# Moving a memory branch (norm, keys, values of two layers) to the top of a three-network program

## The chip, the cores and the metric

The kernel runs on one core of one Trainium2 chip. The metric is device microseconds of one execution; the time before is the median of three. A core has TensorE (matrix products into PSUM, in fp32 or fp32r here), VectorE (DVE), ScalarE (ACT), GpSimd (POOL, which here only starts transfers) and SyncE (SP, which only starts weight transfers). The engines run their own instruction lists in order and meet only at semaphores.

## What is computed

Three small transformer networks stand one behind the other on x, 256 tokens by 1024 channels. The second one has two layers (a fox layer of forget attention, then a conv layer), and each of them also attends to a memory `mem` that doesn't depend on x:

```python
def second_block(x, mem, norm_mix, norm_mem, ...):
    h = x
    for i in range(DEPTH):                      # 2
        u = rms_norm_2(h, norm_mix[i])
        m = rms_norm_2(mem, norm_mem[i])
        mk, mv = jnp.split(m @ w_mem_kv[i], 2, axis=-1)     # 1024 x 512
        ...                                     # fox (i = 0) or conv (i = 1) mix of u, and mq
        mem_out = memory_attention(mq, mk, mv, g_mq[i], g_mk[i])
        h = h + jnp.concatenate([mix, mem_out], axis=-1) @ w_out
        ...
```

`rms_norm_2(mem, g)` is mem times one factor for each token times a gain for each channel, so the token factors are the same for both layers. The first network has adaptive norms: its shifts, scales and gates come from `c` through a matrix `ada_w` of 36 groups of 512 columns, four quarters (512 KB each) a group; the first layer's first norm needs groups 0 to 3.

## The kernel before

x lies in SBUF with channels on the partitions, as 8 tiles of 128 by 256 tokens. Every fp32 product is made as three fp32r matmuls (high times high, high times low, low times high). A chunk is 1 MB of weights, 128 by 2048. SP loads chunks into a ring of 4; ScalarE copies one into `whi` (L1619), VectorE subtracts to get `wlo` (L2409), TensorE multiplies with both, 48 matmuls of 256 columns for a chunk. `split_to` runs up to 3 chunks ahead of the one in use.

A norm is a chain over three engines: ScalarE squares x into T (`squares`), TensorE sums over channels with a column of ones as 32 one-column matmuls (`stat`), ScalarE takes the root (`root`), VectorE the reciprocal (`rinv`), TensorE turns it to a row, ScalarE copies it out (`rows_out`), TensorE broadcasts it over the partitions (`bcast`), VectorE scales (`scaled_rows`), ScalarE makes the high halves (`halves`), VectorE the low ones (`lower`). `heat` puts matmuls on a tile `warm` without a use for their result in between: 4 in the statistics, 18 after the broadcast. Ahead of a feed-forward network each engine waits at a fence for the others.

The program is one fixed order for each engine, written out in the classes Pe, Act, Dve, Pool and Sp. `network()` (L431) does `start`, then `need_mod(0, 1)`, which runs adaLN groups 0 to 3: VectorE sums the weighted rows of each quarter as the GpSimd queue's three buffers (`rring`, "raws") bring them (`ada`, L2391), TensorE adds over partitions (`ada_sums`, 4 products of one column, 8 matmuls), VectorE adds the bias. Then come the first network, `final_norm`, `fox`, a feed-forward network, `conv_layer`, `moe`, `moba` and `cross`.

Around the change: in `fox` and `conv_layer` the GpSimd queue waits for the fence (`after`), then loads a table `ex` and `mem` into the working area AF; the engines run a norm of mem, keys (`lin`) and values (`lin_nat`), and the keys' own factors for each head (`pair_stat`, `head_norm`). In fox the statistics of x stand behind these products, without `heat`; in the conv layer the whole norm of x does. Then x's own chunks begin. In `moba` the table `ex` is loaded a third time together with two others.

Of the kernel before, what the change touches and what calls it, by code (L numbers as in the profile page):

```python
# [28 lines left out]
def const_table():  # L29
# [105 lines left out]
LOADS = ("cst", "small", "x", "pos", "ex0", "mem0", "oh", "ex1", "mem1", "ex3", "rot3", "pool3", "mem3")  # L135
# [34 lines left out]
class Net:  # L170


    def __init__(self, nc, ctx, dram, out, count):
# [21 lines left out]
        self.warm = sb("warm", [P, S], F32R)  # L195
# [8 lines left out]
        self.moes = sb("moes", [P, 8, 16])  # L204
# [22 lines left out]
    def lay(self):  # L227
# [3 lines left out]

        af = Arena(self.AF)
        self.h_CU, self.h_GB = af.take(4, S), af.take(4, S)
        self.h_q0, self.h_kv0 = af.take(2, S), af.take(2, S)
        self.h_Cs, self.h_Sn, self.h_ang, self.h_kk = [af.take(S) for _ in range(4)]
        self.h_qn, self.h_qr = af.take(4, S), af.take(2, S)
        self.h_kn, self.h_vn = af.take(4, S), af.take(2, 512)
        self.h_posi = af.take(S)
        ar = Arena(self.AR)
        ar.n = af.n  # L240
        self.hqh, self.hql, self.hkh, self.hkl = ar.take(2, S), ar.take(2, S), ar.take(1, S), ar.take(1, S)
        assert ar.n <= self.AF.shape[1]
# [8 lines left out]
        self.n_pt, self.n_cs, self.n_gT = af.take(512), af.take(2, 16), af.take(S)  # L251

        af = Arena(self.AF)
        self.x_ex = af.take(1536)[0:24, :]
        keep = af.n
        self.x_q = af.take(6, S)
        af.take(512)
        af.n = keep
        self.m_xm = af.take(8, S)
        self.m_mk, self.m_mv = af.take(2, S), af.take(2, 256)  # L260
        after = af.n
# [4 lines left out]
        af.n = after  # L266
# [10 lines left out]
        af.take(1536)  # L277
# [95 lines left out]
class Side:  # L373
# [58 lines left out]
    def network(self):  # L432
        self.start()
        for l in range(2):
            for j in range(2):
                key = ("ff", l, j)
                self.need_mod(l, 7 if j else 1)
                self.norm((key, "n"), self.N.X, ("mod", l, 2 * j))
# [15 lines left out]
        self.finish_all()  # L454

# [9 lines left out]
class Pe(Side):  # L465
# [93 lines left out]
    def heat(self, n):  # L559

        b = self.take(("heat", self.heats))
        self.heats += 1
        w = self.N.warm
        for _ in range(2 * n):
            self.mm(b[:, 0:S], w[:, 0:P], w[:, :], True, True)

    def norm(self, key, X, which, n=8, T=None):
        T = self.N.T if T is None else T
        self.stat(key, [T[:, k, :] for k in range(n)], heat=2)
        self.rows_of(key, 1)  # L570
        self.bcast(key, self.N.ones[0:1, :])
        self.heat(9)
# [488 lines left out]
    def head_norm(self, key, x, n):  # L1061
        N = self.N
        self.rinv(key, [N.T[:, k, :] for k in range(n)], G=2 * n)
        for k in range(n):
            self.bcast(key, N.x_ex[0:2 * n, k * P:(k + 1) * P], ("bc", k), k == n - 1)
# [11 lines left out]
    def pair_bcast(self, key):  # L1077
        for k in range(2):
            self.bcast(key, self.N.x_ex[0:4, k * P:(k + 1) * P], ("bc", k), k == 1)

    def mem_kv(self, i):
        N = self.N
        self.norm(("mem", i), N.m_xm, ("V", "norm_mem_2", i))
        self.lin(("mem", i, "k"), [(0, "w_mem_kv_2", (i,), 0, 8, (0, 256))], ("mem", i))
        self.lin_nat(("mem", i, "v"), [(0, "w_mem_kv_2", (i,), 0, 8, (256, 256))], ("mem", i))
        self.mark(("mem", i, "in"))
        self.wait_ge("ld_ex0" if i == 0 else "ld_ex1", 16)
        self.head_norm(("mk", i), N.m_mk, 2)

    def mem_heads(self, i, mq, mqkey):  # L1090
        N = self.N

        def ready(h):
            self.wait_ge("dve", (mqkey, "h", h // 2))
            self.wait_ge("dve", (("mk", i), "h", h // 2))
        return Heads(("mem", i), MEM, at=12, q=lambda h: [mq[rows(h), h // 2, :]], k=lambda h: [N.m_mk[rows(h), h // 2, :]],
                     v=lambda h, kb: N.m_mv[:, kb, h * 64:h * 64 + 64], ready=ready,
                     vready=lambda h: self.wait_ge("act", ("mem", i, "v", 1)))
# [2555 lines left out]
```

## Time and profile before

| | us |
|---|---|
| median of 3 runs (3596.22 to 3599.97) | 3598.55 |
| the profiled execution | 3605.26 |
| its span, first to last instruction | 3603.4 |
| TensorE busy | 3291.7 (91%) |
| VectorE busy | 2306.6 (64%) |
| ScalarE busy | 1685.5 (47%) |

Times in the rows below are microseconds from the start of the span unless they say ns. In a timeline a row is a start, a duration, an engine, a line of the kernel, an operation, what it writes and reads, and how often; in brackets stands how long the engine had been idle before it and what ended that. A row of a stretch gives its length, the busy us and instructions of PE, PEld, DVE, ACT and POOL, the granted clock, the DMA engines' busy share and GB/s; a row of a queue its packets, MB and share. A busy TensorE counts overlapping matmuls as one stretch. The granted clock is a share of 2.4 GHz: 1.00 or 0.50, in between for a stretch with both.

### The profile page before, as it was taken

What the parts mean: (1) busy time and instruction counts of PE and PEld (TensorE: products, weight loads), DVE (VectorE), ACT (ScalarE), POOL (GpSimd) and SP (SyncE); (2) the same over time, 40 slices, a digit from 0 to 9 for tenths busy, and PEclk for the clock granted to TensorE, in tenths of its full rate; (3) what the DMA queues carried; (4) which work ended last, traced back from release to release, by engine and by line L of the source; (5) the groups of instructions that cost most, each with busy time, mean ns of one, the idle gap of its engine ahead of it and who ended that gap; (6) DMA issues with size and microseconds to landing.
All of it is one profiled execution on the core that took longest, in us unless ns stands there. A gap on an engine that the chain in (4) does not pass through costs nothing. (4 is left out here: it accounts for less than half of the span.)

```text
span 3603.4 us, 49674 instructions
## 1 busy us (share of the span) xinstructions
PE 3291.7 (91%) x21314; PEld 2982.2 (83%) x21314; DVE 2306.6 (64%) x2636; ACT 1685.5 (47%) x1866; POOL 86.9 (2%) x168
## 2 busy tenths in 40 slices
PE   3998999999989989999826899999999999999999
PEld 3998899999879978799815778778778778889899
DVE  4775577675445543444385678778788787654575
ACT  2334333434324344343302567667667666534453
POOL 1010001010000000000000000000000000000000
PEclk9998899999879978899766899999999999998999
DMA  6784378585214632145311589789798898633253
GB/s 225 263 292 154 119 264 291 208 286 189 95 47 164 211 110 97 59 176 182 110 38 37 192 309 358 303 320 343 292 346 321 304 356 308 246 106 106 100 182 117
DMA packets 112604, 741.05 MB, mean 206 GB/s; under 512 B 12588, under 2 KB 12588, under 8 KB 32224
## 3 DMA queue, kind: packets, MB, share of 16 engines
q1 hardware_dynamic: 89424, 651.21, 49.0%
q0 software_dynamic: 22928, 86.27, 7.0%
q8 instruction: 184, 3.01, 0.3%
q14 instruction: 68, 0.56, 0.0%
HBM read 736.38 MB, written 1.05 MB: 205 GB/s over the span
## 5 line engine op out<-in xcount | busy, mean ns | idle before, releaser
L2409 DVE TENSOR_TENSOR wlo<-ring,whi 128x2048 fp32r<-128x2048 f32 x620 | 1419.3, 2291 | 562.6 <-ACT whi L1619 562.2
L1619 ACT ACTIVATE whi<-ring 128x2048 fp32r<-128x2048 f32 x620 | 1184.8, 1913 | 347.0 <-issue 221.7
L473 PE MATMUL ps<-whi,AR 128*128 128x512 f32 x2692 | 873.9, 400 | 0.1
L473 PE MATMUL ps<-hh,whi 128*128 128x256 f32 x2768 | 798.3, 288 | 9.1 <-DVE wlo L2409 6.8
L473 PE MATMUL ps<-hl,whi 128*128 128x256 f32 x2768 | 791.6, 286 | 0.0
L473 PE MATMUL ps<-hh,wlo 128*128 128x256 f32 x2768 | 791.1, 286 | 0.0
L473 PEld LDWEIGHTS ps<-whi,AR 128*128 128x128 f32 x2692 | 506.6, 188 | 118.4 <-issue 1.6
L473 PEld LDWEIGHTS ps<-hh,whi 128*128 128x128 f32 x2768 | 538.5, 195 | 11.5 <-DVE wlo L2409 7.1
L473 PEld LDWEIGHTS ps<-hl,whi 128*128 128x128 f32 x2768 | 538.3, 194 | 0.5
L473 PEld LDWEIGHTS ps<-hh,wlo 128*128 128x128 f32 x2768 | 537.5, 194 | 0.6
L473 PE MATMUL ps<-wlo,AR 128*128 128x512 f32 x1346 | 532.6, 396 | 0.0
L472 PE MATMUL ps<-AR,whi 128*128 128x256 f32 x2112 | 377.6, 280 | 0.0
L472 PEld LDWEIGHTS ps<-AR,whi 128*128 128x128 f32 x2112 | 325.0, 189 | 0.0
L473 PEld LDWEIGHTS ps<-wlo,AR 128*128 128x128 f32 x1346 | 253.7, 188 | 55.7
L472 PE MATMUL ps<-AR,wlo 128*128 128x256 f32 x1056 | 297.3, 282 | 0.0
L472 PEld LDWEIGHTS ps<-AR,wlo 128*128 128x128 f32 x1056 | 198.9, 188 | 0.0
L2391 DVE SCALAR_TENSOR_TENSOR cv<-rring,ca,cv 128x512 f32<-128x512 f32 x238 | 178.8, 751 | 22.8 <-DMA rring<-in_r 7.9
L1607 ACT ACTIVATE AR<-gf 128x512 fp32r<-128x512 f32 x66 | 41.8, 633 | 252.1 <-DVE gf L2382 252.1
L1607 ACT ACTIVATE cv<-ps,att 128x256 f32<-128x256 f32 (+1 forms) x144 | 60.5, 425 | 208.8 <-DVE att L2400 208.8
L473 PE MATMUL ps<-AF 64*128 64x128 f32 (+4 forms) x456 | 138.6, 415 | 3.1 <-DVE AF L2391 1.8
L482 PE MATMUL ps<-cst,cv 128*128 128x128 f32 x228 | 42.9, 306 | 103.3 <-ACT cv L1607 95.4
L1607 ACT ACTIVATE gs<-ps 128x512 f32<-128x512 f32 x55 | 32.8, 597 | 209.0 <-PE ps L473 209.0
(197 smaller groups left out, 3492.4 us busy)
## 6 DMA issues: line engine op xcount, KB each, us to landing
ring<-in_w SPq DMA_DIRECT2D x620, 1024.0 KB, 4.9
rring<-in_r POOLq DMA_DIRECT2D x151, 512.0 KB, 4.9
AF<-in_mem POOLq DMA_DIRECT2D x3, 1024.0 KB, 5.2
X<-in_x POOLq DMA_DIRECT2D x1, 1024.0 KB, 13.5
AF<-in_cst POOLq DMA_DIRECT2D x1, 1024.0 KB, 6.0
y_out<-X SPq DMA_DIRECT2D x1, 1024.0 KB, 3.9
cst<-in_cst POOLq DMA_DIRECT2D x1, 478.0 KB, 7.5
AF<-in_cst POOLq DMA_DIRECT2D x3, 144.0 KB, 3.0
```

What stands on the lines that cost most here:

```text
L472: return self.e.matmul(out, l, r, start=start, stop=stop, skip_group_check=True)
L473: return self.e.matmul(out, l, r, start=start, stop=stop)
L482: return self.e.transpose(out, in_, self.N.ident[0:n, 0:n])
L1607: self.e.activation(out, in_, f, **kw).then_inc(*self.up(*keys))
L1619: self.e.activation(N.whi[:, c % HB, :], N.ring[:, c % RING, :], ACT.Copy).then_inc(N.sem["hi"], 1)
L2391: self.e.scalar_tensor_tensor(out=out, in0=a, scalar=s, in1=b, op0=op0, op1=op1).then_inc(*self.up(*keys))
L2409: self.e.tensor_tensor(N.wlo[:, c % HB, :], N.ring[:, c % RING, :], N.whi[:, c % HB, :].bitcast(F32), ALU.subtract).then_inc(N.sem["lo"], 1)
```

## The change

The memory branch of both layers leaves `fox` and `conv_layer` and stands in a new `memory()` at the top, between `start` and the first layer. It takes adaLN groups 0 to 3 in, in an order of its own, and the token factors of the first layer's norm, whose scaling (`scale`) stays where the norm was. mem is squared and its factors made once. Keys and values of both layers stay in the last 2048 columns of AF until they are used. GpSimd loads mem ahead of the first raws and x behind them, SP waits for mem ahead of the first chunk. The table `ex` becomes a part of the constants that always stay (2 heads' pairs are enough), `warm` shrinks to 128 columns and is read twice, and some tiles move or share a place. The core of the diff:

```diff
+LOADS = ("cst", "small", "x", "mem", "pos", "oh", "rot3", "pool3", "mem3")
-        self.warm = sb("warm", [P, S], F32R)
+        self.warm = sb("warm", [P, P], F32R)
-        self.moes = sb("moes", [P, 8, 16])
+        self.moes = self.att[:, :, :, :].rearrange("p a b c -> p (a b c)")[:, 0:128].rearrange("p (a b) -> p a b", a=8)
     def network(self):
         self.start()
+        self.memory()
...
-                self.norm((key, "n"), self.N.X, ("mod", l, 2 * j))
+                (self.scale if (key, "n") == FIRST else self.norm)((key, "n"), self.N.X, ("mod", l, 2 * j))
# TensorE
-            self.mm(b[:, 0:S], w[:, 0:P], w[:, :], True, True)
+            self.mm(b[:, 0:S], w[:, :], w[:, :].unsqueeze(1).to_broadcast([P, 2, P]), True, True)
+    def factors(self, key, tiles, heat=2):
+        self.stat(key, tiles, heat=heat)
+        self.rows_of(key, 1)
+        self.bcast(key, self.N.ones[0:1, :])
+    def memory(self):
+        N = self.N
+        self.base, self.span = 0, 8
+        for g in range(4):
+            self.ada(g, 0)
+            self.ada(g, 1)
+        self.adan = 4
+        self.factors("mem", [N.s_tm[:, k, :] for k in range(8)], 0)
+        self.ada_sums(0)
+        for i in range(2):
+            self.lin(("mem", i, "k"), [(0, "w_mem_kv_2", (i,), 0, 8, (0, 256))], ("mem", i), hh=N.s_mh, hl=N.s_ml)
+            self.lin_nat(("mem", i, "v"), [(0, "w_mem_kv_2", (i,), 0, 8, (256, 256))], ("mem", i), hh=N.s_mh, hl=N.s_ml)
+            self.mark(("mem", i, "in"))
+            self.ada_sums(1 + i)
+            self.pair_stat(f"mk{i}")
+            self.pair_rows(f"mk{i}")
+            self.pair_bcast(f"mk{i}")
+        self.factors(FIRST, [N.T[:, k, :] for k in range(8)])
+        self.ada_sums(3)
+        self.base, self.span = 4, 4
     def fox(self):
...
-        self.norm(("mem", 0), N.m_xm, ("V", "norm_mem_2", 0))
-        self.lin(("mem", 0, "k"), [(0, "w_mem_kv_2", (0,), 0, 8, (0, 256))], ("mem", 0))
-        self.lin_nat(("mem", 0, "v"), [(0, "w_mem_kv_2", (0,), 0, 8, (256, 256))], ("mem", 0))
-        self.mark(("mem", 0, "in"))
-        self.wait_ge("ld_ex0", 16)
-        self.pair_stat("mk0")
-        self.stat("fox", [N.T[:, k, :] for k in range(8)])
-        self.pair_rows("mk0")
-        self.rows_of("fox", 1)
-        self.bcast("fox", N.ones[0:1, :])
-        self.pair_bcast("mk0")
+        self.norm("fox", N.X, ("V", "norm_mix_2", 0))
     def conv_layer(self):
-        self.mem_kv(1)
         self.norm("cv", N.X, ("V", "norm_mix_2", 1))
# ScalarE
+    def memory(self):
+        N = self.N
+        self.adan = 4
+        self.squares("mem", N.s_xm, 8, lambda k: self.wait_ge("ld_mem", 16), N.s_tm)
+        self.root("mem", 1024)
+        self.rows_out("mem")
+
+        def keys(i):
+            self.copy_out(("mem", i, "k"), N.m_mk[i])
+            self.pair_squares(f"mk{i}", N.m_mk[i], "act", ("mem", i, "k"))
+            self.copy_nat(("mem", i, "v"), lambda tb: N.m_mv[i][:, tb, :])
+
+        self.halves(("mem", 0), N.s_tm, N.s_mh, 8)
+        self.split_to(1)
+        keys(0)
+        self.wait_ge("mm", ("mem", 0, "in"))
+        self.halves(("mem", 1), N.s_tm, N.s_mh, 8)
+        self.split_to(3)
+        self.root("mk0", 64, 4)
+        self.rows_out("mk0", 4)
+        keys(1)
+        self.squares(FIRST, N.X, 8, lambda k: self.wait_ge("ld_x", 16), N.T)
+        self.root("mk1", 64, 4)
+        self.rows_out("mk1", 4)
+        self.rinv(FIRST, 8 * P)
+        self.chunks += 4
# VectorE
     def start(self):
-        self.wait_ge("ld_x", 16)
+    def memory(self):
+        N = self.N
+        self.adan = 4
+
+        def scaled(i):
+            self.wait_ge("mm", ("mem", "bc"))
...
+        self.ada(0, 0)
+        self.wait_ge("ld_mem", 16)
+        self.rinv("mem")
+        self.ada(0, 1)
+        scaled(0)
+        self.lower(("mem", 0), N.s_tm, N.s_ml, N.s_mh, 8)
+        self.split_to(0)
+        self.ada(1, 0)
+        self.split_to(1)
+        scaled(1)
+        self.ada_sums(0)
+        self.ada(1, 1)
+        self.wait_ge("mm", ("mem", 0, "in"))
+        self.lower(("mem", 1), N.s_tm, N.s_ml, N.s_mh, 8)
+        self.split_to(3)
+        self.ada_sums(1)
+        self.ada(2, 0)
+        self.rinv("mk0", 4)
+        self.ada(2, 1)
+        self.pair("mk0", N.m_mk[0], N.V("g_mk_2", 0))
+        self.ada_sums(2)
+        self.ada(3, 0)
+        self.rinv("mk1", 4)
+        self.ada(3, 1)
+        self.pair("mk1", N.m_mk[1], N.V("g_mk_2", 1))
+        self.rinv(FIRST)
+        self.wait_ge("ld_x", 16)
+        self.ada_sums(3)
+        self.chunks += 4
# VectorE, hybrid
+        self.wait_ge("act", ("hy", "cos"))
         self.lower("hykvn", N.T[:, 1:2, :], N.hkl, N.hkh, 1)
# GpSimd
+        self.load("mem", N.s_xm, N.dram["mem2"])
+        self.raw_to(RAW)
         self.load("x", N.X[:, :, :], N.dram["x"])
-        self.raw_to(RAW)
     def fox(self):
         self.after()
-        self.table("ex0", N.x_ex, N.cat["ex"][0], 1536, 24)
-        self.load("mem0", N.m_xm, N.dram["mem2"])
     def conv_layer(self):
-        self.after()
-        self.table("ex1", N.x_ex, N.cat["ex"][0], 1536, 24)
-        self.load("mem1", N.m_xm, N.dram["mem2"])
+        self.fence()
     def moba(self):
-        self.table("ex3", N.x_ex, N.cat["ex"][0], 1536, 24)
# SP
+        self.wait_ge("ld_mem", 16)
```

## Rows read from the trace of the kernel before

**Rows 1.** The page's busy tenths of TensorE in 40 slices of 90 us.
```profile
PE   3998999999989989999826899999999999999999
```

**Rows 2.** Timeline of the start, all engines.
```profile
16.02 2.19 ACT L1607 ACTIVATE T<-X 128x512 f32<-128x512 f32 x4 [4.82 <-DMA X<-in_x]
...
19.21 0.49 DVE L2386 TENSOR_SCALAR cv<-rring,ca 128x512 f32<-128x512 f32 x1 [18.20 <-DMA rring<-in_r]
...
28.57 4.03 DVE L2391 SCALAR_TENSOR_TENSOR cv<-rring,ca,cv 128x512 f32<-128x512 f32 x5
...
53.35 1.87 PE L473 MATMUL ps<-ones,cv 128*128 128x1 f32 x8 [7.79 <-DVE cv L2391]
...
62.94 0.26 ACT L1607 ACTIVATE st<-ps,cst 128x2 f32<-128x2 f32 x1 [43.44 <-PE ps L472]
...
65.84 3.22 DVE L2391 SCALAR_TENSOR_TENSOR T<-X,gain,ps 128x256 f32<-128x256 f32 x8 [2.44 <-PE ps L473]
...
74.32 8.89 DVE L2409 TENSOR_TENSOR wlo<-ring,whi 128x2048 fp32r<-128x2048 f32 x4 [2.09 <-ACT whi L1619]
...
76.67 0.58 PE L473 MATMUL ps<-hh,whi 128*128 128x256 f32 x1 [6.81 <-DVE wlo L2409]
```

**Rows 3.** DMA queues in 5.5-6, 10-12, 18-20; landing of mem's loads.
```profile
q0 software_dynamic: 16, 0.12, 57.8%
...
q1 hardware_dynamic: 53, 0.43, 52.0%
q0 software_dynamic: 63, 0.39, 46.4%
...
q0 software_dynamic: 233, 0.82, 102.9%
...
DMA to landing us min/median/max: 5.1/5.2/6.9
```

**Rows 4.** Timelines of VectorE, ScalarE and TensorE in the fox layer.
```profile
1286.45 3.22 DVE L2391 SCALAR_TENSOR_TENSOR X<-X,sm,ps 128x256 f32<-128x256 f32 x8 [2.36 <-PE ps L473]
...
1312.46 2.77 DVE L2382 TENSOR_TENSOR hl<-T,hh 128x256 fp32r<-128x256 f32 x8
...
1297.76 2.19 ACT L1607 ACTIVATE T<-AF 128x512 f32<-128x512 f32 x4 [12.61 <-DMA AF<-in_mem]
...
1313.22 0.33 PE L473 MATMUL ps<-hh,whi 128*128 128x256 f32 x1
...
1338.01 0.37 PE L473 MATMUL ps<-hh,whi 128*12 128x256 f32 x1 [2.03 <-DVE hl L2382]
```

**Rows 5.** The same three timelines in the conv layer.
```profile
1718.65 2.73 DVE L2382 TENSOR_TENSOR X<-X,ps 128x256 f32<-128x256 f32 x8
...
1727.85 2.19 ACT L1607 ACTIVATE T<-AF 128x512 f32<-128x512 f32 x4 [11.44 <-DMA AF<-in_mem]
...
1743.29 0.34 PE L473 MATMUL ps<-hh,whi 128*128 128x256 f32 x1
...
1775.45 0.41 PE L473 MATMUL ps<-hh,whi 128*128 128x256 f32 x1
```

**Rows 6.** Timelines of ScalarE and TensorE at the third network's first norm.
```profile
3109.25 2.19 ACT L1607 ACTIVATE T<-X 128x512 f32<-128x512 f32 x4 [5.96 <-DVE X L2382]
...
3122.59 0.33 PE L473 MATMUL ps<-hh,whi 128*128 128x256 f32 x1
```

**Rows 7.** Four stretches: busy time of each engine, granted clock, transfers.
```profile
120.00:140.00 20.00, 20.00 (x169) 19.92 (x169) 15.54 (x18) 7.83 (x6) 2.11 (x4) 1.00 0.81 283
...
76.00:81.00 5.00, 4.33 (x20) 4.34 (x21) 5.00 (x4) 4.90 (x4) 0.00 (x0) 1.00 0.64 236
...
1330.00:1340.00 10.00, 7.22 (x27) 4.51 (x27) 5.85 (x17) 5.97 (x12) 0.00 (x0) 0.50 0.00 0
...
1760.00:1768.00 8.00, 8.00 (x36) 7.35 (x36) 0.96 (x2) 0.79 (x2) 0.00 (x0) 0.50 0.00 0
```

More of the change, by code:

```diff
@@ L264, in lay @@
         self.x_oh = af.take(1536)[0:12, :]
-        af.n = after
+        assert af.n <= free
+        af = Arena(self.AF)
         self.c_U, self.c_acc, self.c_mq = af.take(6, S), af.take(6, S), af.take(2, S)
@@ L564, in heat, with scale @@
         for _ in range(2 * n):
-            self.mm(b[:, 0:S], w[:, 0:P], w[:, :], True, True)
+            self.mm(b[:, 0:S], w[:, :], w[:, :].unsqueeze(1).to_broadcast([P, 2, P]), True, True)
     def norm(self, key, X, which, n=8, T=None):
         T = self.N.T if T is None else T
-        self.stat(key, [T[:, k, :] for k in range(n)], heat=2)
+        self.factors(key, [T[:, k, :] for k in range(n)])
+        self.heat(9)
+    def factors(self, key, tiles, heat=2):
+        self.stat(key, tiles, heat=heat)
         self.rows_of(key, 1)
         self.bcast(key, self.N.ones[0:1, :])
-        self.heat(9)
+    def scale(self, key, X, which):
+        pass
     def final_norm(self):
@@ L1685, in norm, with scale @@
         if which is not None:
-            if which[0] == "mod":
-                self.wait_ge("dve", ("part", which[1], 3 * which[2]))
-            self.halves(key, T, N.hh, n, gain_of(N, which)[1])
+            self.scale(key, X, which, n, T)
+    def scale(self, key, X, which, n=8, T=None):
+        N = self.N
+        if which[0] == "mod":
+            self.wait_ge("dve", ("part", which[1], 3 * which[2]))
+        self.halves(key, N.T if T is None else T, N.hh, n, gain_of(N, which)[1])
     def final_norm(self):
@@ L1996, in fox @@
         self.wait_ge("act", f)
-        self.norm(("mem", 0), N.m_xm, ("V", "norm_mem_2", 0), ready=lambda k: self.wait_ge("ld_mem0", 16))
-        self.wait_ge("dve", (("mem", 0), "h", 7))
-        self.squares("fox", N.X, 8, self.ready_x, N.T)
-        self.chunk()
-        self.copy_out(("mem", 0, "k"), N.m_mk)
-        self.pair_squares("mk0", N.m_mk, "act", ("mem", 0, "k"))
-        self.chunk()
-        self.copy_nat(("mem", 0, "v"), lambda tb: N.m_mv[:, tb, :])
-        self.root("mk0", 64, 4)
-        self.root("fox", 1024)
-        self.rows_out("mk0", 4)
-        self.rows_out("fox")
-        self.wait_ge("mm", ("mem", 0, "in"))
-        self.halves("fox", N.T, N.hh, 8)
+        self.norm("fox", N.X, ("V", "norm_mix_2", 0))
         self.chunk()
@@ L2446, in norm, with scale @@
     def norm(self, key, X, which, n=8):
+        self.rinv(key)
+        self.scale(key, X, which, n)
+    def scale(self, key, X, which, n=8):
         N = self.N
-        self.rinv(key)
         gain, shift = gain_of(N, which)
@@ L2989, in fox @@
         self.wait_ge("dve", f)
-        self.wait_ge("ld_mem0", 16)
-        self.norm(("mem", 0), N.m_xm, ("V", "norm_mem_2", 0))
-        self.chunk()
-        self.chunk()
+        self.norm("fox", N.X, ("V", "norm_mix_2", 0))
         gq = self.scaled(N.V("fox_g_q_2", 0), 20, 0.125)
@@ L2997, in fox @@
         self.wait_ge("dve", self.here())
-        self.rinv("mk0", 4)
-        self.rinv("fox")
-        self.scaled_rows("fox", N.T, N.X, N.V("norm_mix_2", 0), 8, lambda k: ("fox", "n", k))
-        self.wait_ge("mm", ("mem", 0, "in"))
-        self.lower("fox", N.T, N.hl, N.hh, 8)
-        self.pair("mk0", N.m_mk, N.V("g_mk_2", 0))
         self.chunk()
@@ L3450, in ada, with memory @@
         self.use_raws(2)
+    def memory(self):
+        for g in range(4):
+            self.ada(g, 0)
+            self.ada(g, 1)
+        self.adan = 4
     def use_raws(self, n):
@@ L3460, in norm @@
         pass
+    scale = norm
     def final_norm(self):
```

94 lines of the change are left out of this document (35 added, 59 removed).

## The prediction

> **What bounds the kernel now.** I read the busy slices of the page first: TensorE is busy nearly throughout, except in the first slice, 3 tenths of 90 us [rows 1]. So work that leaves TensorE's path later on is a gain, and what matters is whether the start can take it up. The start is read in order of time [rows 2]: x is squared at 16.02, the first adaLN quarter is summed by VectorE at 19.21, four groups of quarters follow, the last 8 small matmuls of a group run at 53.35, and only then does TensorE take the token statistics of the first layer, so that their square root comes at 62.94, the scaling at 65.84 and the first matmul of the network at 76.67. The two later places: the second network's first layer (fox) [rows 4] and its conv layer [rows 5]; in each, a norm of mem, loaded just then, stands ahead of the norm of x. What ends last in both is one serial chain: load, squares (ScalarE), 32 one-column matmuls, root, turn, broadcast, scale, lower halves, first matmul.
>
> **Two prices used throughout.** A 256-column matmul takes 0.118 us at the full rate (169 in 20.00 us) and 0.217 at the low one (20 in 4.33 us) [rows 7]. At 76 to 81 us the granted clock is written as 1.00, yet the spacing is that of 1.2 GHz; where the record says 0.50, in 1760 to 1768, 36 small ones fill 8.00 us [rows 7]. A chunk's 48 matmuls thus take 5.7 us warm; started cold, with 20 at the low rate, 4.3 + 28 x 0.118 = 7.7 us.
>
> **Fox.** Before: x is final at 1286.45 + 3.22 = 1289.7; squares of mem start at 1297.76; its first matmul is at 1313.22; the first matmul on x at 1338.01 [rows 4]. After: squares of x can start at 1289.9 and the same chain follows. From squares to first matmul it takes 15.5 us here (1297.76 to 1313.22), and 13.3 in the third network's first stage, where no transfer is waited for (3109.25 to 3122.59) [rows 6]. TensorE is now idle for less long ahead of it, so I take 14.5: 1304.4, which is 33.6 earlier (bounds 32.6 and 34.8). The 18 warming matmuls, which the old path left out ahead of x, now precede it; the 24 matmuls of the first chunk, begun at 1338 with 0.50 granted [rows 7], run at the full rate: 24 x 0.1 = 2.4, taken (bounds 0 and 2.6). Together 36.0. Next late is nothing new: the four chunks in hand are those for x, split ahead by both engines.
>
> **Conv.** x is final at 1718.65 + 2.73 = 1721.4; mem's squares at 1727.85, its first matmul 1743.29, x's first at 1775.45 [rows 5]. After: squares at 1721.6, plus 13.3 to 15.4, take 14.4: 1736.0, 39.4 earlier; a warmer first chunk adds 0 to 1.1, take 0.5. Together 39.9 (bounds 38.4 and 41.6). The depthwise convolution behind it hangs on these chunks and moves with them.
>
> **The third network** loses one of three table loads, but its first matmul (3122.59) follows the scaling and not a load [rows 6]: nothing. Also nothing: the new addresses; the extra VectorE wait for the cosine in the hybrid layer (ScalarE makes it ahead of the copies that the same step waits for anyway); the gate and router tiles laid on others, with no wait added. The warming matmuls now read 128 columns twice; the same 256 columns pass, taken as equal (see the rivals).
>
> **The start, walked engine by engine.** All this is new and in order on each engine; VectorE: quarters 0-1, 2-3, scale mem, lower, split 0, quarters, split 1, scale mem again, quarters, (mem 0 through TensorE), lower, splits 2-3, quarters, reciprocal of key 0, and so on.
> 1. Loads. The GpSimd queue's first bytes flow at about 5.5 us (0.12 MB by 6) and alone it carries 0.82 MB in 2 us [rows 3]. Constants (now 606 KB), small table and mem are 2.06 MB: 5.0 us, with landing 11.3. The SP queue now waits for this. Sharing gives each queue about half, 0.39 and 0.43 MB in 2 us [rows 3]; so raws 0 to 2 land at 12.5, 13.8, 16.3, x at 21, raw 3, queued behind it, at 23.8; weight chunk 0 near 18.
> 2. Statistics of mem: squares at 11.3; at the low rate 32 of the 36 matmuls that fill 8.00 us [rows 7] take about 7.2, from 11.6 on, so root at 18.8, reciprocal 19.2. VectorE, with quarters 0-1 done by 15.7 (4 steps a pair; 5 steps take 4.03 us [rows 2], so 3.2 a pair), takes quarter 2 to 20.8 and waits for raw 3: 25.4.
> 3. Scale 3.2 [rows 2], lower 2.8 [rows 4], first split 2.2 (four take 8.89 [rows 2]): 33.7. TensorE's keys of layer 0 start at 33.8, cold, 7.7: 41.5; values 5.7: 47.3.
> 4. VectorE meanwhile: pair 36.9, split 39.2, scale 42.4, pair 45.8; it then waits for 47.3. ScalarE's halves and two splits end at 54.0, VectorE's lower at 51.0 and its two splits at 56.6, pair 60.0, reciprocal 60.2.
> 5. TensorE stands from 49 until that reciprocal: its program turns and broadcasts key 0's factors ahead of layer 1. This takes about 3.1 (one factor, root to scale, 62.94 to 65.84 [rows 2], with a second broadcast). Layer 1 starts at 63.3, cold: 7.7 + 5.7 + the group's sums 1.0 (half of the 1.87 at 53.35, as warm) = 77.7.
> 6. VectorE has the sums of group 2 in its order ahead of group 3, and group 2's matmuls stand behind layer 1 on TensorE: it is held from 65 to 77.9. Then a pair 81.1, reciprocal of key 1, turn, broadcast 84.4.
> 7. TensorE now takes x's statistics, cold, 7.8: 92.2; root to broadcast 2.9 [rows 2]: 95.1; the sums of group 3 take 1.9 (53.35), VectorE adds: 97.5. Before, scaling at 65.84 led to the first matmul at 76.67, 10.8 later [rows 2]: the same steps give 108.3.
> So the first layer starts 31.6 later. Bounds: with no wait at all VectorE's own work (16 quarters 24.3, two scalings 6.4, two lowers 5.5, four splits 8.9, small ones 2.5) from 12.5 ends at 60.1, and with step 7's tail without the statistics (some 16) the first matmul would come at 76: a price of 0. At the other end, later raws (3), no warm matmul (4 in the two layers), and slower handovers (2): 41.
>
> **Two pages weighed.** The rows show a 1 MB load landing 5.1 us or more after its issue, and both queues sharing [rows 3]. The Trainium skill (DMA: Bandwidth & Descriptors, the anatomy of one SWDGE transfer) fits a transfer as 2.0 us plus its bytes over 436 GB/s, and says that engines alternate between queues by packet; the second agrees with the rows. By the first, mem would land near 9.2 and the start would cost some 2 us less; the rows decide.
> The rows have TensorE at the low rate when it resumes after standing (0.217 us a matmul from 76 on, 0.50 granted up to 1340 and from 1760 on [rows 7]). The Trainium skill (TensorE: Matmul & The Clock Gate, HAM oscillation) says the same of kernels whose work comes in islands, and advises keeping it together; it speaks against this start, in which layer 0, layer 1 and x's statistics are three islands. Were all three warm, the start would cost about 7 us less.
>
> **Sum.** Removed 36.0 + 39.9 = 75.9; added 31.6; net 44.3 off the profiled 3605.26 (span 3603.4). That execution is 6.7 above the median 3598.55; the difference belongs to stages, so it is taken off the median: 3554.
>
> **Rivals.** (A) Forecast, 3542 to 3568, 0.64. (B) The start is cheaper, about 15: the waits of steps 5 and 6 are shorter, because TensorE or the loads come earlier than I walked. For: VectorE's own work could end at 60. Against: the order of both programs makes these waits. 3598.6 - 75.9 + 15 = 3538; 0.12. (C) The start costs about 50, since the raws and the weights delay each other all through, not only raw 3: 3573; 0.14. (D) The two removed passes hid something, such as weight loads or splits, so that about 50 of the 75.9 come: 3580; it includes the case that the change does not do what it says in one of the layers. Against: the queue is idle there, and both splits run ahead. 0.06. (E) Slower: the warming matmuls, fed now by a repeated 128-column block, take longer. Thirteen blocks of 18 remain right ahead of the first matmul of their stages, in the chain. At 0.217 each, doubled, they cost 3.9 us a block, 51 in all, against 44 gained: slower than before from about 1.9 times their present length, 3605 at double. Against: the same columns pass, and no row shows a pattern slowing a matmul. 0.04.
>
> **Numbers.** About 0.2%, 7 us, is what a measurement can tell. A and B lie below it, C and D nearly all: faster 0.93, same 0.03 (tails of C to E), slower 0.04. The range takes the bounds of A, half of B and most of C's near side: 3540 to 3572.
>
> **What would show it.** In the changed profile: the first matmul on mem near 34, a stand of TensorE of about 11 us before 63 that ends with a reciprocal, VectorE held until about 78, the network's first matmul near 108; fox's first matmul on x 14 to 15 us after the squares, near 1336; conv's near 1732; warming matmuls of the same length. A first network matmul before 95 or after 120 proves the walk wrong, a gap between squares and first matmul over 16 in fox or conv proves the removal wrong.

## The result and the profile after

| | before | changed |
|---|---|---|
| median, us | 3597.39 (3594.31 to 3599.97, 4 runs) | 3547.41 (3538.64 to 3555.22, 4 runs) |
| the profiled execution | 3605.26 | 3542.27 |
| its span | 3603.4 | 3540.4 |
| first matmul of the first network | 76.67 | 105.54 |

The ratio of changed to before is 0.9861, with a 95% interval of 0.9832 to 0.9889: the change saves 50 us by the medians and 63 between the two profiled executions. The forecast was 3554, within 3540 to 3572.

The page of the changed kernel, busy tenths of TensorE in 40 slices of 89 us, to be held against [rows 1]: the first slice has risen from 3 to 6, since keys and values of both layers run there, and the second has fallen from 9 to 8, since the first network starts inside it.
```profile
PE   6899999999999999999808999999999999999999
```

The timeline of the changed kernel's start, which answers to [rows 2] (start, duration, engine, line, operation, count; in brackets the idle time before and its end). L481, L482, L491, L2402, L2411, L2417, L2429 and L1620 are L472, L473, L482, L2382, L2391, L2397, L2409 and L1607 of before.
```profile
9.49 2.19 ACT L1620 ACTIVATE AF<-AF 128x512 f32<-128x512 f32 x4 [1.23 <-DMA AF<-in_mem]
10.27 6.96 PE L481 MATMUL ps<-ones,AF 128*128 128x1 f32 x32 [10.27 <-ACT AF L1620]
...
17.63 0.17 DVE L2417 RECIPROCAL st<-st 128x2 f32<-128x2 f32 x1 [3.90 <-ACT st L1620]
...
22.00 1.54 DVE L2411 SCALAR_TENSOR_TENSOR cv<-rring,ca,cv 128x512 f32<-128x512 f32 x2 [2.57 <-DMA rring<-in_r]
...
31.61 0.80 PE L482 MATMUL ps<-AR,whi 128*128 128x256 f32 x2 [6.15 <-DVE wlo L2429]
...
57.40 0.59 PE L491 MATMUL ps<-cst,st 128*4 128x128 f32 x2 [10.70 <-DVE st L2417]
...
60.45 0.80 PE L482 MATMUL ps<-AR,whi 128*128 128x256 f32 x2
...
75.55 0.16 DVE L2402 TENSOR_TENSOR mod<-ps,sm 128x4 f32<-128x4 f32 x1 [11.40 <-PE ps L482]
...
81.75 3.57 PE L481 MATMUL ps<-ones,T 128*128 128x1 f32 x16
...
94.71 3.22 DVE L2411 SCALAR_TENSOR_TENSOR T<-X,gain,ps 128x256 f32<-128x256 f32 x8
...
105.54 0.58 PE L482 MATMUL ps<-hh,whi 128*128 128x256 f32 x1 [11.34 <-DVE wlo L2429]
```
What is to be seen: the chain has two long stands of one engine, TensorE's 10.70 ahead of 57.40 and VectorE's 11.40 ahead of 75.55. How much of each is due to the order alone is what the experiments below find out.

The fox layer of the changed kernel, which answers to [rows 4]: final scaling of the first network, squares of x, scaling, first matmul on x.
```profile
1312.55 3.23 DVE L2411 SCALAR_TENSOR_TENSOR X<-X,sm,ps 128x256 f32<-128x256 f32 x8 [2.36 <-PE ps L482]
...
1315.86 2.19 ACT L1620 ACTIVATE T<-X 128x512 f32<-128x512 f32 x4 [4.62 <-DVE X L2411]
...
1329.04 0.41 PE L482 MATMUL ps<-hh,whi 128*12 128x256 f32 x1
```
The same of the conv layer, for [rows 5].
```profile
1700.55 2.73 DVE L2402 TENSOR_TENSOR X<-X,ps 128x256 f32<-128x256 f32 x8
...
1703.36 2.19 ACT L1620 ACTIVATE T<-X 128x512 f32<-128x512 f32 x4 [5.05 <-DVE X L2402]
...
1718.12 0.41 PE L482 MATMUL ps<-hh,whi 128*128 128x256 f32 x1
```
From the final scaling's start to the first matmul on x, fox takes 1329.04 - 1312.55 = 16.5 us, against 1338.01 - 1286.45 = 51.6 before: 35.1 less. From x's last addition to the first matmul on x, conv takes 1718.12 - 1700.55 = 17.6, against 56.8: 39.2 less.

### The profile page after: what moved, and what is told of

Read it like the earlier page. It is cut to its first block, busy times and chain, and to the rows that moved or that the text cites. A ratio compares the mean times of both kernels' runs of the same rounds, so it can differ in the third digit from the quotient of the medians.

```text
span 3540.4 us, 49498 instructions
## 1 busy us (share of the span) xinstructions
PE 3262.7 (92%) x21238; PEld 2953.9 (83%) x21238; DVE 2306.3 (65%) x2635; ACT 1682.4 (48%) x1860; POOL 84.8 (2%) x164
## 4 chain that ended last, share of the span: by engine, by line
PE 78%; DVE 6%; ACT 2%; issue 1%; DMA 0%; DVEq 0%; ACTq 0%; POOLq 0%
PE ps L482 62%; PE ps L481 13%; DVE AF L2411 3%; PE ps L491 2%; DVE wlo L2429 1%; ACT whi L1632 1%; DVE X L2402 0%; DVE hl L2402 0%; DVE AR L3300 0%; DVE T L2402 0%; ACT hh L1620 0%; DVE X L2411 0%; ACT rT L1620 0%; DVE cv L2411 0%; DVE AR L2408 0%
## 5 line engine op out<-in xcount | busy, mean ns | idle before, releaser
L2429 DVE TENSOR_TENSOR wlo<-ring,whi 128x2048 fp32r<-128x2048 f32 x620 | 1419.3, 2291 | 552.2 <-ACT whi L1632 551.9
L482 PE MATMUL ps<-whi,AR 128*128 128x512 f32 (+1 forms) x2756 | 885.5, 397 | 0.0
L482 PE MATMUL ps<-hh,whi 128*128 128x256 f32 (+1 forms) x2736 | 785.6, 287 | 11.5 <-DVE wlo L2429 11.3
L482 PE MATMUL ps<-hl,whi 128*128 128x256 f32 (+1 forms) x2736 | 778.9, 285 | 0.0
L482 PE MATMUL ps<-hh,wlo 128*128 128x256 f32 (+1 forms) x2736 | 778.2, 284 | 0.0
L482 PEld LDWEIGHTS ps<-whi,AR 128*128 128x128 f32 x2756 | 516.3, 188 | 118.3 <-issue 1.6
L482 PE MATMUL ps<-wlo,AR 128*128 128x512 f32 (+1 forms) x1378 | 541.4, 393 | 0.0
L482 PEld LDWEIGHTS ps<-hh,whi 128*128 128x128 f32 (+1 forms) x2736 | 529.2, 193 | 12.6 <-DVE wlo L2429 11.4
L482 PEld LDWEIGHTS ps<-hl,whi 128*128 128x128 f32 (+1 forms) x2736 | 529.3, 193 | 0.3
L482 PEld LDWEIGHTS ps<-hh,wlo 128*128 128x128 f32 (+1 forms) x2736 | 528.5, 193 | 0.3
L481 PE MATMUL ps<-AR,whi 128*128 128x256 f32 x2112 | 378.3, 280 | 0.0
L481 PEld LDWEIGHTS ps<-AR,whi 128*128 128x128 f32 x2112 | 325.5, 189 | 0.0
L482 PEld LDWEIGHTS ps<-wlo,AR 128*128 128x128 f32 x1378 | 259.6, 188 | 55.8
L481 PE MATMUL ps<-AR,wlo 128*128 128x256 f32 x1056 | 297.5, 282 | 0.0
L481 PEld LDWEIGHTS ps<-AR,wlo 128*128 128x128 f32 x1056 | 199.2, 189 | 0.0
L2411 DVE SCALAR_TENSOR_TENSOR cv<-rring,ca,cv 128x512 f32<-128x512 f32 x238 | 178.8, 751 | 25.5 <-DMA rring<-in_r 9.4
L1620 ACT ACTIVATE AR<-gf 128x512 fp32r<-128x512 f32 x66 | 41.8, 633 | 252.3 <-DVE gf L2402 252.3
L1620 ACT ACTIVATE cv<-ps,att 128x256 f32<-128x256 f32 (+1 forms) x144 | 60.6, 426 | 208.4 <-DVE att L2420 208.4
L482 PE MATMUL ps<-AF 64*128 64x128 f32 (+4 forms) x456 | 141.6, 424 | 3.1 <-DVE AF L2411 2.4
L491 PE MATMUL ps<-cst,cv 128*128 128x128 f32 x228 | 42.6, 304 | 101.9 <-ACT cv L1620 93.9
L1620 ACT ACTIVATE gs<-ps 128x512 f32<-128x512 f32 x55 | 32.9, 597 | 209.9 <-PE ps L482 209.9
```

The costliest lines, as they stand in the source:

```text
L481: return self.e.matmul(out, l, r, start=start, stop=stop, skip_group_check=True)
L482: return self.e.matmul(out, l, r, start=start, stop=stop)
L491: return self.e.transpose(out, in_, self.N.ident[0:n, 0:n])
L1620: self.e.activation(out, in_, f, **kw).then_inc(*self.up(*keys))
L2411: self.e.scalar_tensor_tensor(out=out, in0=a, scalar=s, in1=b, op0=op0, op1=op1).then_inc(*self.up(*keys))
L2429: self.e.tensor_tensor(N.wlo[:, c % HB, :], N.ring[:, c % RING, :], N.whi[:, c % HB, :].bitcast(F32), ALU.subtract).then_inc(N.sem["lo"], 1)
```

## Where the time went, by stage

The boundaries are the first network's first matmul, fox's first matmul on x, and the start of one weight split of VectorE near the end of the conv layer, the same one in all kernels; each row is one profiled execution, in us. The last nine, of eight kernels, have the change in fox and conv; they differ from each other by design at the start alone, except the one without warming.

| kernel | to the first matmul | to fox's matmul on x | to the end of conv | to the end |
|---|---|---|---|---|
| before | 76.7 | 1261.3 | 685.4 | 1580.0 |
| before, again | 75.7 | 1254.8 | 684.3 | 1576.9 |
| changed | 105.5 | 1223.5 | 633.1 | 1578.2 |
| changed, again | 104.4 | 1222.1 | 633.3 | 1571.5 |
| sums of group 2 later | 102.9 | 1226.7 | 633.9 | 1575.6 |
| no wait for mem on SP | 110.0 | 1225.7 | 632.6 | 1569.1 |
| key factors behind layer 1 | 96.9 | 1225.2 | 637.0 | 1578.4 |
| x's factors in place | 105.4 | 1219.0 | 639.7 | 1576.3 |
| start reordered | 82.4 | 1220.0 | 640.0 | 1577.7 |
| without mem's work | 68.7 | 1220.9 | 635.8 | 1572.7 |
| without warming in fox | 105.7 | 1222.6 | 641.2 | 1572.5 |

So the start costs 28.9 and the two layers give it back and more; behind the conv layer nothing stands clearly out of the scatter (1569 to 1578, 1575 on average, against 1577 and 1580).

## The experiments

**The theory** is the sum of the prediction: a chain removed in fox and in conv, a chain added at the start whose length is the order of the programs. **The rivals** are that the work at the start costs that much in any order, that the removed passes gave something back (D), that the warming matmuls changed (E), that the place of x's token factors matters, and chance for whatever exceeds the sum.

### The changed kernel and the kernel before, once more

No edit: the changed kernel is timed five times more, and the kernel before as if it were a new one.

> The changed kernel once more, with five rounds, since its four runs lay 17 us apart (3538.6 to 3555.2) where those of before lay 6 apart. Theory S (structure): start 28.9 later, fox 35.0 and 2.6 earlier, conv 40 earlier, 49 in all, so 3548 in the median, and the spread comes from the granted clock in stretches in which TensorE is busy in pieces, such as fox's attention. Then the first matmul of the network stands again at 105.5 and fox and conv give the same lengths to 1 us, while the attention stages differ from the first profile by some us. Theory F (fixed): the 63 us between the first two profiles are all from the change, and the new profile shows the 6.6 us gained inside fox's attention again, and the median goes to 3540.

Measured: 3538.17 (3533.24 to 3539.45, 5 runs) against 3592.5 (3589.63 to 3595.92, 9 runs), ratio 0.985 [0.9837, 0.9864]; span 3531.3. The signs that came are those of theory F, not of S: the median is 3538, and fox's attention, from the first matmul on x, takes 121.6 as in the first profile (121.8). The first matmul of the first network is at 104.42, 1.1 earlier than expected.

> The kernel before, profiled a second time. Its first profile took 130.9 us from fox's first matmul on x to the end of its attention, the changed kernel's two profiles 121.8 and 121.6; 2.6 of the 9.1 are the first chunk at the full clock. Theory S: the other 6.5 are stretches at a low granted clock that come and go, so this profile differs from the first by some us there, without an edit. Theory F: the change removed them by something, then this profile takes 130.9 again to 1 us.

Measured: 3591.51 (8 runs) against 3595.14 (9 runs), ratio 0.9993 [0.9981, 1.0005]; span 3591.8, 11.6 less than that of the first profiled execution, with the same program. The attention of fox is one place where it comes from: 127.2 in place of 130.9, so theory F fails here. Four stretches of it, the first two of before, the other two of before again, which has come to the same place of the program 7.5 us earlier (length, busy us and instructions of PE, PEld, DVE, ACT, POOL, granted clock, DMA share, GB/s):
```profile
1360.00:1380.00 20.00, 20.00 (x161) 18.85 (x159) 9.18 (x10) 9.33 (x14) 0.00 (x0) 1.00 0.40 142
...
1400.00:1420.00 20.00, 20.00 (x126) 17.89 (x124) 7.82 (x12) 9.54 (x19) 0.00 (x0) 0.83 0.18 61
```
```profile
1360.00:1380.00 20.00, 19.54 (x110) 15.63 (x109) 6.73 (x12) 6.78 (x12) 0.00 (x0) 0.81 0.31 106
...
1400.00:1420.00 20.00, 20.00 (x141) 16.86 (x141) 7.63 (x17) 10.09 (x21) 0.00 (x0) 1.00 0.29 106
```
With the same program the granted clock falls below 1.00 in other stretches from execution to execution, though TensorE is busy for 19.5 to 20.0 us of each 20. The changed program does it too: the reordered kernel below, which has the same fox layer, takes 128.2 for this attention. One stretch of it, and the one of the changed kernel at the same distance (60 us) from fox's first matmul on x:
```profile
1362.00:1382.00 20.00, 20.00 (x124) 17.74 (x123) 7.52 (x10) 9.96 (x19) 0.00 (x0) 0.83 0.19 71
```
```profile
1389.00:1409.00 20.00, 20.00 (x142) 16.86 (x141) 8.01 (x12) 9.45 (x20) 0.00 (x0) 1.00 0.29 106
```
So a few us of any difference of two profiles are chance.

### Without mem's work

Keys and values of both layers are constants of 0.5; mem's norm, products and key factors are left out, the rest of the new order stays. TensorE's part of the edit, with its lines on the products joined into one; ScalarE and VectorE lose what belongs to them:
```diff
-        self.factors("mem", [N.s_tm[:, k, :] for k in range(8)], 0)
         self.ada_sums(0)
-        for i in range(2):
-            self.lin(...) ... self.pair_bcast(f"mk{i}")
+        self.ada_sums(1)
+        self.ada_sums(2)
         self.factors(FIRST, [N.T[:, k, :] for k in range(8)])
```


> The memory branch's norm, keys and values are left out altogether (keys and values are set to 0.5, so the attention to memory computes something else); adaLN groups and the first layer's factors stay at the top. It prices the removal apart from the start. Fox and conv should be as in the changed kernel to 1 us. VectorE's quarters run from 10.8 and need some 34 us as before, and root to first matmul follows: first matmul of the network at about 61, 44 earlier than 105.5, so 3503 (3493 to 3513). If the removed passes had hidden something (rival D), or the stages behind take back what they get, it is more than 3515.

Measured: 3510.91 (3499.99 to 3516.1), ratio 0.9779 [0.9764, 0.9794]. Its first network matmul and the wait that I had not counted:
```profile
21.57 1.54 DVE L2381 SCALAR_TENSOR_TENSOR cv<-rring,ca,cv 128x512 f32<-128x512 f32 x2 [6.12 <-DMA rring<-in_r]
```
```profile
68.75 0.58 PE L482 MATMUL ps<-hh,whi 128*128 128x256 f32 x1 [11.33 <-DVE wlo L2399]
```
The start is 7.7 longer than I expected: x, loaded ahead of raw 3, holds VectorE for 6.12, and the next raws for 2.50 and less. The median is 8 above the 3503 expected, within the range given. Two things follow. The stages behind the start take 1220.9 and 635.8, among the values of the kernels with mem's work at the start (1219.0 to 1226.7 and 632.6 to 640.0): nothing of that work is felt later beyond the scatter. And mem's work costs 105.54 - 68.75 = 36.8 in the order that the change has.

### Key factors of layer 0 behind layer 1

TensorE's part; ScalarE's row of layer 0 moves behind the keys of layer 1, and VectorE applies the factors one pair of quarters later.
```diff
+            if i:
+                self.pair_rows("mk0")
+                self.pair_bcast("mk0")
             self.pair_stat(f"mk{i}")
-            self.pair_rows(f"mk{i}")
-            self.pair_bcast(f"mk{i}")
+        self.pair_rows("mk1")
+        self.pair_bcast("mk1")
```


> TensorE takes the turn and broadcast of layer 0's key factors behind layer 1's products instead of ahead of them. By my walk (steps 4 and 5) TensorE stood for 10.7 us only because of this order, and layer 1 could start once its first chunk is split, near 52 instead of 60.45: network's first matmul near 97 to 98, 7 to 9 us less in all. By the rival that the start is bound by VectorE's own work or the quarters' transfers, the first matmul stays within 2 us of 105.5.

Measured: 3530.05 (3527.29 to 3539.41), ratio 0.9825 [0.981, 0.984], against 3538.17 for the changed kernel on the same chip. Layer 1 and the first network of this kernel:
```profile
51.66 0.80 PE L482 MATMUL ps<-AR,whi 128*128 128x256 f32 x2 [5.36 <-DVE wlo L2432]
```
```profile
96.86 0.58 PE L482 MATMUL ps<-hh,whi 128*128 128x256 f32 x1 [11.33 <-DVE wlo L2432]
```
Layer 1 starts at 51.66 in place of 60.45, and all but 0.1 of the 8.8 arrives at the first network (96.86 against 105.54). So the order that step 5 of the walk named was on the path. But the stand did not go away: TensorE still stands for 5.36, now until VectorE has split layer 1's first chunk. Of the 8.8, 5.3 is the half of the stand that was there for the reciprocal alone (10.70 - 5.36), 3.1 is the turn and broadcast (57.40 to 60.45), which are now done behind layer 1 while VectorE is busy, and 0.4 was gained before.

### The sums of group 2 later on VectorE

```diff
-        self.ada_sums(2)
         self.ada(3, 0)
-        self.rinv("mk1", 4)
         self.ada(3, 1)
+        self.ada_sums(2)
+        self.rinv("mk1", 4)
```


> VectorE takes the sums of group 2 behind group 3's quarters and not ahead of them (step 6 of my walk). It no longer stands for 11.4 us behind layer 1. But TensorE's end of layer 1 (75.4), not VectorE, then sets what follows: root of key 1 waits for its squares' sum and for x's squares on ScalarE, to 77.4, so the turn starts about 1 us earlier than 78.70 and the network's first matmul is at 104 to 105 instead of 105.5. If the stand itself were the cost, it would be 97 or less.

Measured: 3541.1 (2 runs), ratio 0.9858 [0.9823, 0.9894]; first matmul at 102.87, 2.7 earlier. But layer 1 ended 1.2 earlier in this execution (its last sums at 73.34 against 74.56), since TensorE's granted clock was 1.00 from 64 us on, where the changed kernel's profile has 0.50 from 64 to 66 and 0.89 from 66 to 68. So the order gave about 1.4, close to the 1 expected. VectorE's 11.40 in step 6 is mostly waiting that nobody needed: only the pair of quarters that stood behind it, before key 1's reciprocal, was on the path.

### SP doesn't wait for mem

```diff
-        self.wait_ge("ld_mem", 16)
         for i in range(len(self.count.specs)):
```


> SP no longer waits for mem ahead of the first weights. Both queues then share from the start, about half each. By that, 2.06 MB of constants and mem land near 15 instead of 9.4, root and reciprocal come near 23 instead of 17.6, and raw 3 near 24 instead of 22: scaling of mem starts at about 27 instead of 23.4, network's first matmul 3 to 4 us later, 108 to 110. If the queues do not take from each other, or weights matter at once, it is within 1 us of 105.5 or earlier.

Measured: 3539.49 (2 runs), ratio 0.9854 [0.9818, 0.9889]. Its squares of mem and its first network matmul:
```profile
17.58 2.19 ACT L1620 ACTIVATE AF<-AF 128x512 f32<-128x512 f32 x4 [4.84 <-DMA AF<-in_mem]
```
```profile
109.99 0.58 PE L482 MATMUL ps<-hh,whi 128*128 128x256 f32 x1 [11.34 <-DVE wlo L2429]
```
Mem comes later than the 15 expected. The new wait brings it 8.1 earlier (9.49 against 17.58), and the first network 4.5 earlier. The times don't show this gain: the ratio to before is 0.9854 without the wait and 0.985 and 0.9861 with it. Of the other 3.6, 2.5 is lost by the scaling of mem: this kernel has its quarters all landed by then and goes from mem's reciprocal (25.71) to the scaling (29.07) in 3.4, where the changed kernel takes 5.8 (17.63 to 23.45) with its wait for raw 3. The last 1.1 is the clock again: layer 1 starts 5.9 later here (66.33 against 60.45) and its last sums only 4.4 later (79.00 against 74.56), for the granted clock rises about 3 us after layer 1's start here (0.70 from 68 to 70), and about 6 us after it in the changed kernel (0.89 from 66 to 68). So the wait for mem is worth nearer 5.6, the delay of the scaling (29.07 against 23.45), than 4.5.

### x's token factors back in their place

TensorE's part and the call; ScalarE's squares and root and VectorE's reciprocal go back into the norm likewise.
```diff
-        self.factors(FIRST, [N.T[:, k, :] for k in range(8)])
         self.ada_sums(3)
...
-                (self.scale if (key, "n") == FIRST else self.norm)((key, "n"), self.N.X, ("mod", l, 2 * j))
+                self.norm((key, "n"), self.N.X, ("mod", l, 2 * j))
```


> The changed kernel with the first layer's token factors (squares, statistics, root, reciprocal, row, broadcast) back inside the first layer's norm, behind the sums of adaLN group 3; memory stays at the top. Theory: in this order of the start the place of the factors is worth nothing. TensorE is free at the same moment, 82, and does the same two things in the other order: sums of group 3 by 84.2 (1.9), statistics of x 84.2 to 92.1 (7.8 cold), reciprocal near 92.4, broadcast, scaling of x near 95.0 against 94.71, first matmul of the first network near 105.8 against 105.54. The 18 warming matmuls that come back with the norm make its first chunk up to 2.4 us shorter. Time within 3 us of the changed kernel. Rival: having the factors ahead of the last columns is a gain of its own; then the first matmul comes 2 to 8 us later, near 108 to 113.

Measured: 3542.63 (2 runs), ratio 0.9863 [0.9834, 0.9891]. The sums of group 3, x's statistics and the first network matmul of this kernel:
```profile
82.11 1.86 PE L482 MATMUL ps<-ones,cv 128*128 128x1 f32 x8 [0.67 <-DVE cv L2408]
83.83 3.55 PE L481 MATMUL ps<-ones,T 128*128 128x1 f32 x16
...
105.42 0.58 PE L482 MATMUL ps<-hh,whi 128*128 128x256 f32 x1 [6.81 <-DVE wlo L2426]
```
105.42 against 105.54: with memory at the top, having the factors ahead of the last columns is worth nothing. Both are TensorE's work, one behind the other. VectorE's last quarter is done at 82.0, 0.1 before TensorE's sums start; TensorE stands 0.67 for it, and that is all that the quarters cost.

### The start reordered

All is computed. TensorE takes x's statistics where it waited for layer 0's second splits, both reciprocals and their rows behind the keys of layer 1, the broadcast of key 1 last; VectorE takes three quarters ahead of the second scaling and puts the factors of key 1 behind the scaling of x. TensorE's part:
```diff
-        for i in range(2):
-            ...
-        self.factors(FIRST, [N.T[:, k, :] for k in range(8)])
+        keys(0)
+        vals(0)
+        self.ada_sums(0)
+        self.ada_sums(1)
+        self.pair_stat("mk0")
+        self.stat(FIRST, [N.T[:, k, :] for k in range(8)])
+        keys(1)
+        self.pair_rows("mk0")
+        self.rows_of(FIRST, 1)
+        self.pair_bcast("mk0")
+        vals(1)
+        self.ada_sums(2)
+        self.pair_stat("mk1")
+        self.bcast(FIRST, N.ones[0:1, :])
         self.ada_sums(3)
+        self.pair_rows("mk1")
+        self.pair_bcast("mk1")
```


> The start in another order, everything computed: quarter 3 of group 0 behind the first split, x's squares and statistics in TensorE's gap between the layers, both factor rows behind layer 1's keys, group 2's sums behind group 3's quarters, layer 1's key factors applied behind the first layer's scaling. By my walk VectorE's own work then sets the start: scaling of mem at 20, layer 0 at 28, layer 1 at 49, last quarter at 64.5, first matmul of the network at 78 (75 to 85), that is 27 us below the changed kernel: 3520 (3508 to 3530). If what the start costs is the work itself and not the waits, the first matmul is later than 95 and the time above 3535.

Measured: 3520.54 (3515.35 to 3523.78), ratio 0.9797 [0.9784, 0.9811]; first matmul at 82.36. VectorE's last quarter ends at 68.6 and not at 64.5, which is 4.1 of the 4.4 missing to the 78 expected; VectorE stands three times for raws on the way there, for 2.25, 3.21 and 1.28. Its x statistics and the first of these waits:
```profile
44.99 5.93 PE L486 MATMUL ps<-ones,T 128*128 128x1 f32 x32
```
```profile
41.59 1.54 DVE L2429 SCALAR_TENSOR_TENSOR cv<-rring,ca,cv 128x512 f32<-128x512 f32 x2 [2.25 <-DMA rring<-in_r]
```
The same work costs 82.36 - 68.75 = 13.6 in this order and 36.8 in that of the change, 23.2 less. Layer 1 starts at 50.78 and not 60.45, and its last sums come at 66.75 and not 74.56: 7.8. From there to the first network it takes 15.6 and not 31.0, 15.4 less, since x's statistics and key 1's factors no longer stand in between. The kernel's ratio to before is 0.9797, against 0.985 for the changed kernel on the same chip.

### Fox's norm without warming

The 4 warming matmuls in x's statistics and the 18 behind the broadcast are left out in fox.
```diff
-        self.norm("fox", N.X, ("V", "norm_mix_2", 0))
+        self.factors("fox", [N.T[:, k, :] for k in range(8)], 0)
```


> In the fox layer the 4 and the 18 warming matmuls around x's factors are left out, the rest is the changed kernel. It prices the term of 2.4 us for a first chunk on the full clock. Expected: squares to first matmul gets shorter by at most 1 (the 4 matmuls in the statistics), the first 24 matmuls are 0.21 apart instead of 0.12, so they take 5.1 us instead of 2.9, and the attention starts 1.5 to 3 us later. If the clock rises without them, nothing moves.

Measured: 3543.81 (2 runs), ratio 0.9866 [0.983, 0.9901]. The first two matmuls on x, and the stretch around them:
```profile
1328.28 0.37 PE L482 MATMUL ps<-hh,whi 128*12 128x256 f32 x1 [3.74 <-DVE hl L2402]
1328.44 0.41 PE L482 MATMUL ps<-hl,whi 128*12 128x256 f32 x1
```
```profile
1328.00:1333.00 5.00, 4.72 (x23) 3.06 (x24) 4.90 (x11) 2.04 (x2) 0.00 (x0) 0.50 0.01 3
```
With them, in the changed kernel:
```profile
1329.00:1334.00 5.00, 5.00 (x43) 4.29 (x41) 4.47 (x10) 3.42 (x3) 0.00 (x0) 0.96 0.00 0
```
23 against 43 matmuls in 5 us, 0.50 against 0.96 granted. The first 64 matmuls on x take 9.9 us, and 7.9 with warming, so the warm first chunks are worth 2.0 here (1.7 to 2.2 against the eight profiles with warming); the 2.4 of the sum was near. The first matmul comes 1.1 sooner after the squares (12.1 against 13.2), so that about half of it is paid again ahead of the chunk. The attention ends 2.5 later after the first matmul; the other 0.5 is within its scatter. The Trainium skill (TensorE: Matmul & The Clock Gate, HAM oscillation) has islands of work start at the low rate unless the work is kept together; this trace agrees, here and in the three islands of the start: TensorE is at 1.2 GHz at the first keys (21 matmuls in 4.40 us from 31.60), at layer 1 (23 from 60.00 to 65.00, 0.50 granted) and at x's statistics (0.50 granted from 81.75 to 85.00).

## Why the prediction was right

**Fox.** Predicted 33.6 and 2.4. Measured 35.1 and 2.5 (the offset to the trace of before grows by that much in the first chunks). The squares start 0.1 behind x, as said. From there to the first matmul it takes 13.2, not 14.5. It would be wrong to learn from this that the third network's 13.3 [rows 6] was the better row: the eight profiles with the change and with warming have 12.8 to 13.3 five times and 15.4 to 15.5 three times, 14.0 on average. The difference is TensorE's clock at x's statistics. The stretch around the start of the squares, where it takes 13.2 (the changed kernel) and where it takes 15.5 (key factors behind layer 1):
```profile
1314.00:1319.00 5.00, 4.75 (x35) 4.55 (x34) 1.78 (x5) 2.19 (x4) 0.52 (x1) 0.83 0.06 15
```
```profile
1305.00:1310.00 5.00, 5.00 (x25) 4.81 (x23) 1.55 (x4) 2.19 (x4) 0.52 (x1) 0.50 0.06 15
```
The forecast's bounds for this stretch, 13.3 and 15.5, are nearly these two cases, and its 14.5 is near their mean.

**Conv.** Predicted 39.4 and 0.5. Measured 39.2 and 0.8; from squares to first matmul 14.8 for the 14.4 taken. By the depthwise convolution, 40.0 together.

**The start.** Predicted 31.6, measured 28.9. Step by step:

| | walked | measured |
|---|---|---|
| mem squared | 11.3 | 9.49 |
| mem's reciprocal | 19.2 | 17.63 |
| quarters behind raw 3 done | 25.4 | 23.5 |
| keys of layer 0 start | 33.8 | 31.61 |
| TensorE stands ahead of key 0's reciprocal | 11 | 10.70 |
| layer 1 starts | 63.3 | 60.45 |
| VectorE is released | 77.9 | 75.55 |
| x's statistics start | 84.4 | 81.75 |
| scaling of x | 97.5 | 94.71 |
| first network matmul | 108.3 | 105.54 |

The error is made in step 1, where mem lands 1.8 too late, and little is added: 2.2 at the first keys, 2.8 at the end. I took the GpSimd queue's first bytes at 5.5 us from [rows 3], but there SP's weights had the DMA engines first. With SP held back, the changed kernel's queue moves bytes from before 3 us on and is at its full rate from 4 (1 us stretches, last two columns DMA share and GB/s):
```profile
3.00:4.00 1.00, 0.00 (x0) 0.00 (x0) 0.00 (x0) 0.00 (x0) 1.00 (x2) 1.00 0.66 179
4.00:5.00 1.00, 0.00 (x0) 0.00 (x0) 0.00 (x0) 0.00 (x0) 1.00 (x3) 1.00 1.00 405
```
I took the queue's rate from a stretch in which it runs alone, but its start from one in which it doesn't. The Trainium skill (DMA: Bandwidth & Descriptors, the anatomy of one SWDGE transfer) has a fit of 2.0 us plus bytes over 436 GB/s for one transfer. An estimate by it, all 2.06 MB taken from mem's issue at 2.45 on, gives 9.2 for this landing, and the measured 9.49 is nearer to that than to my 11.3.

**The sum.** The mechanisms read from the two profiles give 28.9 - 35.1 - 2.5 - 40.0 = -48.7 us; forecast -44.3. The difference of the medians is -50.0, and -54.3 when it was timed again; that of the profiles -63.0.

These terms are themselves uncertain by some us. Read from the second profile of each kernel they are 28.7 - 33.9 - 2.0 - 37.1 = -44.3. That this is the forecast to the tenth is luck. The removed chain of conv was 2.8 shorter in that execution of before. Its stretch with x's statistics, in before and in before again:
```profile
1758.00:1768.00 10.00, 9.54 (x40) 8.40 (x39) 0.96 (x2) 2.45 (x5) 0.00 (x0) 0.50 0.02 7
```
```profile
1750.00:1760.00 10.00, 9.11 (x42) 8.15 (x42) 1.08 (x3) 2.46 (x6) 0.00 (x0) 0.57 0.00 0
```
What exceeds 48.7 in the first profiles lies in the first network (2.8), fox's attention (6.6), the rest up to the end of conv (3.1) and the last stages (1.8). The two executions of before differ by 6.5 in the first network and by 3.7 in fox's attention (127.2 against 130.9). Not all of it is settled: to the end of conv the nine executions with the change take 636 on average and the two of before 685, 49 less, of which 41 (mean of the two readings) to 42.5 is read from rows. Some 4 of the other 6 to 8 are in fox's attention, where seven of the nine take 120.6 to 122.2 us, the reordered kernel 128.2 and the one without warming 124.3. The reordered kernel shows that the clock can fall there with the change too; whether it falls less often because of the change or by chance stays open. So the forecast was right in its mechanisms and near in the size of each (2.7 too long at the start, 1.6 too little in fox, by the first profiles); the measured gain is 6 to 10 us above it, and a part of that has no named cause.

**The rivals.** (B) a cheaper start: false in this order, since the waits of steps 5 and 6 were there with their lengths (10.70 and 11.40), though VectorE's cost only 1.4; but the reordered kernel shows that most of it was the order and not the work, with a start only 5.7 behind that of before. Its time of 3520.5 lies below B's 3538, which had a start of 15. (C) a start of 50: false; raws and weights delayed VectorE at raw 3, by 2.57, and later by at most 2.84 where it had time. (D) something hidden under the removed passes: false, since fox gives 35.1 + 2.5 and conv 40.0 (33.9 + 2.0 and 37.1 by the second profiles) of the 75.9 read off. (E) longer warming matmuls: false. The group of warming matmuls, before and changed (count, busy us, mean ns of one):
```profile
L473 PE MATMUL ps<-warm 128*128 128x256 f32 x330 | 75.7, 408 | 0.0
```
```profile
L482 PE MATMUL ps<-warm 128*128 128x256 f32 x290 | 65.8, 404 | 0.0
```
Reading 128 columns twice takes as long as reading 256 once: a block of 18 at 0.50 granted takes 4.21 us in both kernels.

## What to carry to other kernels

Work taken out of a serial chain gives the chain's whole length, and that can be read from two rows, x's last write and its first matmul; two profiles of the same kernel may give it 1 to 3 us apart. What it costs in its new place has to be walked there engine by engine: between the order as made and a better one lay 23 us of 37. The moves priced alone are a reciprocal, turn and broadcast that stood ahead of independent products (8.7) and sums taken too early by VectorE (1.4); the other 13 come from the reordered kernel as a whole and weren't split further. A long stand is not a price: VectorE's 11.40 cost 1.4, and TensorE's 10.70 gave back only half of itself. And two readings of the same term, from two executions, tell more than the tenths of one.

## What was not expected of the hardware

- The same program differed by 11.6 us between two profiled executions (3603.4 and 3591.8), with the granted clock at 1.00 in one and 0.81 in the other from 1360 to 1380 us.
- At the very start the granted clock says 1.00 while the matmuls are 0.21 us apart, those of 1.2 GHz; so there the spacing and not the granted clock tells the rate. The stretch at the first keys of the changed kernel, 21 matmuls in 4.40 us:
```profile
31.60:36.00 4.40, 4.39 (x21) 4.39 (x22) 4.22 (x5) 0.00 (x0) 1.05 (x2) 1.00 0.72 257
```
- Holding SP's queue back until mem had landed didn't delay the first products: the start gained 4.5 us. The transfers together run at 418 to 428 GB/s from 8 to 16 us without the wait and at 421 from 10 to 20 with it, so the wait changes which bytes come first and not how many.
